# Norm sums from two fp32r parts, and the first four projection tiles split twice and stored once, in an encoder layer

## What is computed

```python
def _layer(x, ...):
    h = _rms(x, norm1_g)
    proj = h @ w_in                                  # 1024 -> 1792: q 512, k 128, v 128, GLU 2 x 512
    q, k, v, c = jnp.split(proj, [...], axis=-1)
    q = _rms(q.reshape(B, T, N_HEADS, HEAD_DIM), q_norm_g)
    k = _rms(k.reshape(B, T, N_KV_HEADS, HEAD_DIM), k_norm_g)
    attn = _window_attention(q, k, v, attn_sink)     # 128-query blocks against 384 keys
    a, gate = jnp.split(c, 2, axis=-1)
    u = _dwconv(a * jax.nn.sigmoid(gate), conv_dw_w, conv_dw_b)          # 31 taps
    u = jax.nn.silu(_layernorm(u, conv_ln_g, conv_ln_b))                 # over 512 channels
    x = x + jnp.concatenate([attn, u], axis=-1) @ w_out
    h2 = _rms(x, norm2_g)                                                # over 1024 channels
    g = jax.nn.silu(_dwconv(h2 @ ffn_w_gate, ffn_dw_w, ffn_dw_b))
    return x + (g * (h2 @ ffn_w_up)) @ ffn_w_down
```

## Time and profile before

| | us |
|---|---|
| runs | 2664.71, 2662.30, 2663.15 |
| median | 2663.15 |
| the profiled execution | 2662.67 |
| its span in the trace | 2660.9 |
| TensorE busy | 2631.4 (99%) |
| VectorE busy | 1820.6 (68%) |
| ScalarE busy | 1258.5 (47%) |
| GpSimd busy | 192.8 (7%) |

### The profile page before, as it was taken

The page is one execution under the profiler, slowest core; times in us unless marked ns, Lnnn a source line. Parts: engine busy times, 40 slices in busy tenths (PEclk is TensorE's granted clock), DMA queues, the critical chain, the costliest instruction groups (busy, mean ns, idle before and its releaser), DMA issues.

```text
span 2660.9 us, 35240 instructions
## 1 busy us (share of the span) xinstructions
PE 2631.4 (99%) x13191; PEld 2337.7 (88%) x13191; DVE 1820.6 (68%) x3020; ACT 1258.5 (47%) x2031; POOL 192.8 (7%) x332
## 2 busy tenths in 40 slices
PE   8999999999999999999999999999999999999998
PEld 6777777788889988889998889998899999999998
DVE  4775658787686876676876677876257576765764
ACT  6345464566454447345446345446144333533432
POOL 0110021100110000010000010000000000000001
PEclk9999999999999999999999999999999999999999
DMA  9967679633843444843443853433745521222211
GB/s 332 349 227 249 249 280 361 231 128 125 298 165 117 156 132 135 290 167 115 157 136 123 291 169 120 157 129 132 284 157 174 177 64 60 68 65 63 68 52 66
DMA packets 138761, 453.73 MB, mean 171 GB/s; under 512 B 24449, under 2 KB 37121, under 8 KB 121953
## 3 DMA queue, kind: packets, MB, share of 16 engines
q1 hardware_dynamic: 111616, 349.17, 39.0%
q0 software_dynamic: 26976, 102.32, 10.5%
HBM read 362.63 MB, written 88.79 MB: 170 GB/s over the span
## 4 chain that ended last, share of the span: by engine, by line
PE 93%; DVE 3%; issue 1%; DMA 1%; ACT 1%; SPq 0%; POOL 0%; DVEq 0%; ACTq 0%; POOLq 0%
PE bank L2131 31%; PE bank L2147 16%; PE bank L2277 12%; PE bank L2083 12%; PE bank L2117 8%; PE bank L2293 7%; PE bank L2231 2%; PE bank L2209 2%; PE bank L2220 2%; DMA wraw<-w_in_t 1%; DVE weights L1561 0%; PE bank L2176 0%; DMA weight_scratch<-weights 0%; ACT weights L1147 0%; ACT part_hi L1404 0%
## 5 line engine op out<-in xcount | busy, mean ns | idle before, releaser
L2131 PE MATMUL bank<-hw_hi,weights 128*128 128x440 f32 (+1 forms) x2816 | 812.2, 365 | 0.0
L2131 PEld LDWEIGHTS bank<-hw_hi,weights 128*128 128x128 f32 x2816 | 530.0, 188 | 47.9 <-issue 12.9
L2131 PE MATMUL bank<-hw_lo,weights 128*128 128x440 f32 (+1 forms) x1408 | 510.8, 363 | 0.0
L2147 PE MATMUL bank<-mid,weights 128*128 128x438 f32 x2112 | 431.9, 364 | 0.0
L1561 DVE TENSOR_TENSOR weights<-wraw,weights 128x1024 fp32r<-128x1024 f32 x286 | 348.8, 1220 | 117.0 <-ACT weights L1147 116.8
L2147 PEld LDWEIGHTS bank<-mid,weights 128*128 128x128 f32 x2112 | 396.0, 189 | 33.3 <-issue 7.6
L1147 ACT ACTIVATE weights<-wraw 128x1024 fp32r<-128x1024 f32 x286 | 301.5, 1054 | 256.9 <-DMA wraw<-w_down_t 171.2
L1668 DVE SCALAR_TENSOR_TENSOR cc<-win,par,cc 128x512 f32<-128x512 f32 x600 | 414.5, 744 | 0.0
L2083 PE MATMUL bank<-h_hi,weights 128*128 128x512 f32 x1104 | 358.6, 398 | 2.9 <-DVE weights L1561 2.9
L2131 PEld LDWEIGHTS bank<-hw_lo,weights 128*128 128x128 f32 x1408 | 264.4, 188 | 16.6 <-issue 1.0
L2083 PEld LDWEIGHTS bank<-h_hi,weights 128*128 128x128 f32 x1104 | 207.9, 188 | 56.0 <-issue 8.3
(11 more groups left out here) (213 smaller groups left out, 3688.0 us busy)
## 6 DMA issues: line engine op xcount, KB each, us to landing
weights<-weight_scratch SPq DMA_DIRECT2D x88, 1024.0 KB, 5.9
wraw<-w_ffn_t SPq DMA_DIRECT2D x176, 512.0 KB, 3.5
wraw<-w_down_t SPq DMA_DIRECT2D x88, 512.0 KB, 3.5
weight_scratch<-weights POOLq DMA_DIRECT2D x22, 1024.0 KB, 8.3
part_raw<-w_ffn_t SPq DMA_DIRECT2D x88, 256.0 KB, 2.6
part_raw<-w_pass_t SPq DMA_DIRECT2D x44, 256.0 KB, 2.6
cat_hi<-cat_scratch SPq DMA_DIRECT2D x10, 1024.0 KB, 6.6
cat_lo<-cat_scratch SPq DMA_DIRECT2D x10, 1024.0 KB, 9.0
```

Source lines behind the costliest of these rows:

```text
L2131: mm = nc.tensor.matmul(out, l[:, k, :], r[:, k, 1:TC + 1] if s else r[:, k, :], start=(k == 0 and j == 0), stop=(k == KT - 1 and j == 2))
L2147: mm = nc.tensor.matmul(out, l[:, q, :], mid[:, k, part, :], start=(k == 0 and j == 0), stop=(k == FH - 1 and j == 2))
```

## The change

**Norm sums.** A new helper `split_sum` on VectorE follows the last add: it copies `ln_acc` to fp32r (`sum_hi`), and writes `ln_acc` minus `sum_hi` as fp32r in place (`sum_lo`). `sum_hi` has the address of `ln_st`, `sum_lo` that of `ln_acc`. The sum over partitions is then two fp32r matmuls with ones, `sum_parts`. The counters that count adds grow by two. `ones` becomes an fp32r tile, made by a memset and a copy at the start.

```diff
+            def split_sum(signal, n):
+                dve.wait_ge(signal, n)
+                nc.vector.tensor_copy(sum_hi[:], ln_acc[:]).then_inc(signal, 1)
+                dve.wait_ge(signal, n + 1)
+                nc.vector.tensor_tensor(sum_lo[:], ln_acc[:], sum_hi[:].bitcast(F32), ALU.subtract).then_inc(signal, 1)
...
                     nc.vector.tensor_tensor(ln_acc[:], ln_acc[:], cc[:, j, :], ALU.add).then_inc(s_l["added"], 1)
+                if c > 0:
+                    dve.wait_ge(s_l["scaled"], c)
+                    dve.wait_ge(s_h2, KT * c)
+                split_sum(s_l["added"], LN_ADDS * c + CT - 1)
...
                         nc.vector.tensor_tensor(ln_acc[:], ln_acc[:], t[:], ALU.add).then_inc(s_l["sq_added"], 1)
+                    dve.wait_ge(s_l["centred"], c + 1)
+                    split_sum(s_l["sq_added"], n + CT - 1)
...
+                if o == KT - 1:
+                    if c > 0:
+                        dve.wait_ge(s_h2, KT * c)
+                    dve.wait_ge(s_l["scaled"], c + 1)
+                    split_sum(s_n2a, n)
...
+            def sum_parts():
+                nc.tensor.matmul(bank[SHARE][:], ones[:], sum_hi[:], start=True, stop=False)
+                return nc.tensor.matmul(bank[SHARE][:], ones[:], sum_lo[:], start=False, stop=True)
+
             def ln_sum(c):
                 pe.wait_ge(s_shared, SHARED["ln_sum", c] - 1)
-                pe.wait_ge(s_l["added"], (CT - 1) * (c + 1))
-                nc.tensor.matmul(bank[SHARE][:], ones[:], ln_acc[:], start=True, stop=True).then_inc(s_l["sum"], 1)
+                pe.wait_ge(s_l["added"], LN_ADDS * (c + 1))
+                sum_parts().then_inc(s_l["sum"], 1)
```

```diff
+UNSTORED = RING
 WEIGHT = [s[2] + (PROJ if s[0] == "O" else 0) if s[0] in "AO" else None for s in SLOT]
-STORES = [s[0] in "AO" and WEIGHT.index(WEIGHT[n]) == n for n, s in enumerate(SLOT)]
-SPLIT = [s[0] not in "AO" or STORES[n] for n, s in enumerate(SLOT)]
+STORED_BY = [1 if f < UNSTORED else 0 for f in range(PROJ)] + KT * [0]
+STORES = [s[0] in "AO" and s[1] == STORED_BY[WEIGHT[n]] for n, s in enumerate(SLOT)]
+SPLIT = [s[0] not in "AO" or s[1] <= STORED_BY[WEIGHT[n]] for n, s in enumerate(SLOT)]
...
-            store_weight(0)
             for n in range(SLOTS + 1):
```

More of the change, by code:

```diff
@@ L62 @@
 AHEAD = 2
+LN_ADDS, N2_ADDS = CT - 1 + 2, KT - 1 + 2
 NEG = -1e30
@@ L595, in encoder_layer @@
         sq, n2_acc, n2_rs = [ln_a, ln_b], ln_acc, ln_st
+        SUM_AT = R_SIDE + 2 * 4 * GROUP * BAND + 2 * 4 * AT * P + 4 * (TB + 2 * P) + 4 * (BLOCKS + 2) * KV_W + 4 * BAND + \
+            2 * up(4 * (TB + 2 * HALO)) + 4 * CT * TB
+        sum_lo, sum_hi = run(SUM_AT, ("sum_lo", [P, TB], F32R), ("sum_hi", [P, TB], F32R))
         ln_out = [(ln_a, ln_b), (ln_acc, ln_st)]
@@ L1921, in _ @@
             nc.vector.memset(eps[:, 1:2], 1e-5).then_inc(s_set, 1)
-            nc.vector.memset(ones[:], 1.0).then_inc(s_set, 1)
+            nc.vector.memset(ln_a[:, 0:P], 1.0).then_inc(s_set, 1)
+            dve.wait_ge(s_set, 4)
+            nc.vector.tensor_copy(ones[:], ln_a[:, 0:P]).then_inc(s_set, 1)
             dve.wait_ge(s_par, 16)
@@ L2164, in first_sum @@
                 pe.wait_ge(s_x0a, PIECES)
-                nc.tensor.matmul(bank[A_MISC][:], ones[:], x0_acc[:, 0, :], start=True, stop=True).then_inc(s_x0m, 1)
+                nc.tensor.matmul(bank[A_MISC][:], ones[:].bitcast(F32), x0_acc[:, 0, :], start=True, stop=True).then_inc(s_x0m, 1)
             def qk_sum(c):
@@ L2234, in values @@
                 mm.then_inc(s_pv, 1)
+            def sum_parts():
+                nc.tensor.matmul(bank[SHARE][:], ones[:], sum_hi[:], start=True, stop=False)
+                return nc.tensor.matmul(bank[SHARE][:], ones[:], sum_lo[:], start=False, stop=True)
             def ln_sum(c):
                 pe.wait_ge(s_shared, SHARED["ln_sum", c] - 1)
-                pe.wait_ge(s_l["added"], (CT - 1) * (c + 1))
-                nc.tensor.matmul(bank[SHARE][:], ones[:], ln_acc[:], start=True, stop=True).then_inc(s_l["sum"], 1)
+                pe.wait_ge(s_l["added"], LN_ADDS * (c + 1))
+                sum_parts().then_inc(s_l["sum"], 1)
             def ln_var(c):
                 pe.wait_ge(s_shared, SHARED["ln_var", c] - 1)
-                pe.wait_ge(s_l["sq_added"], (CT - 1) * (c + 1))
-                nc.tensor.matmul(bank[SHARE][:], ones[:], ln_acc[:], start=True, stop=True).then_inc(s_l["var"], 1)
+                pe.wait_ge(s_l["sq_added"], LN_ADDS * (c + 1))
+                sum_parts().then_inc(s_l["var"], 1)
             def norm2_sum(c):
                 pe.wait_ge(s_shared, SHARED["norm2", c] - 1)
-                pe.wait_ge(s_n2a, (KT - 1) * (c + 1))
-                nc.tensor.matmul(bank[SHARE][:], ones[:], n2_acc[:], start=True, stop=True).then_inc(s_n2m, 1)
+                pe.wait_ge(s_n2a, N2_ADDS * (c + 1))
+                sum_parts().then_inc(s_n2m, 1)
             def pair_product(k, q, g, p):
```

20 lines of the change are left out of this document (10 added, 10 removed).

## The result

| | before | changed |
|---|---|---|
| median of 14 runs, us | 2664.23 | 2670.97 |
| lowest and highest | 2661.26, 2667.38 | 2662.36, 2679.73 |
| span of the profiled execution | 2660.9 | 2665.5 |

The ratio is 1.0024, with a 95% interval of 1.0015 to 1.0033: some 6.4 us slower. The forecast was 2660.0, a little faster, with 2665.0 as its upper end.

A forecast was written before the change was run, and what follows sets the result against it. TensorE was taken as the bound, busy 2631.4 of 2660.9 us. Moved weight stores -5.0 + 0.2 + 0.6 = -4.2, norm sums +1.3, together -2.9: 2659.8 from the profiled 2662.67, 2660.0 as median; range 2655.5 to 2665.

The forecast's parts named there:

- nine sums with room: Norm sums whose adds end well before the sum starts: each was to save 0.40 us of TensorE, 3.6 in all.
- Slack that is read from a trace: At chunk 1's spread near 134: 1.7 us of token-load delay counted as free, leaving 0.6 us with lower clock.

## What to carry to other kernels

A high and low split in front of a matmul that ends a chain of adds puts two dependent VectorE instructions, 1.3 us here, into that chain to save 0.4 us of TensorE; use it where the adds end that much earlier than the sum, and look at what stands behind the split in VectorE's queue as well as behind the sum. Of the nine sums with room only five kept their saving: a faster sum gains nothing where TensorE's next operand comes from a chain that does not hang on it. Slack that is read from a trace belongs to that trace: if TensorE is to arrive earlier, what comes out of full DMA queues does not, and the slack there shrinks by the gain. Bytes that are moved out of a full stretch should go to one that has room, and it is worth reading the DMA share of the stretch they go to.

## What the runs showed of the hardware

A VectorE copy of 128x512 from fp32 to fp32r took 0.43 us, where a subtraction with two tensors took 0.69. VectorE idled 0.03 us before an instruction that waits on one semaphore, its own last instruction's, 0.10 before one with two waits and 0.13 before one with three. One 512-column matmul stepped by 0.23 in fp32r, and a plain fp32 one by 0.86, in two records.

The lower clock behind a wait of TensorE did not follow from the wait's length alone. After one of 1.59 us the granted clock fell to 0.50 in one place, and stayed at 1.00 after waits of 1.57 and 1.59 in two others. In the pass over pairs near 2612 all 14 traces have the same wait of 1.86 or 1.87 us; in four of them, that of before among them, the clock fell to 0.50 behind it, which cost 1.3 us in that of before, and in ten it stayed at 1.00. A 512 KB token load took 8.8 us in the kernel before and 12.7 in the changed one (the third tile of chunk 1), both at a DMA share of 1.0; with the stores moved out of that stretch it took 9.0.
